# One of two low parts of the expert table's weights made by GpSimd, gathered rows' dot products with x in PSUM, and a ring of three PSUM banks in place of four

## The chip, the cores and the metric

One core of one Trainium2 chip runs the whole program in one launch. The metric is the device time of one execution in microseconds (us), the median over runs of the same kernel. TensorE (PE) does the matmuls, VectorE (DVE), ScalarE (ACT) and GpSimd (POOL) the elementwise work, SyncE (SP) issues most of the DMAs.

## The reference

Two transformer blocks follow each other over 512 tokens of width 1024, all in float32. The change lies in the second half of the first block, a layer of 16384 single-neuron experts (PEER):

```python
def chunk(xc):                                     # 128 tokens
    q = (xc @ wq).reshape(PEER_CHUNK, PEER_HEADS, 2, PEER_HALF)
    s = jnp.einsum('chpd,hpkd->chpk', q, subkeys)
    s1, i1 = lax.top_k(s[:, :, 0], PEER_TOPK)
    s2, i2 = lax.top_k(s[:, :, 1], PEER_TOPK)
    ...
    cs, ci = lax.top_k(cand, PEER_TOPK)
    eidx = jnp.take_along_axis(cidx, ci, axis=-1)  # 128 experts for a token
    g = jax.nn.softmax(cs, axis=-1)
    hid = jnp.einsum('cd,chkd->chk', xc, jnp.take(u_table, eidx, axis=0))
    a = jax.nn.gelu(hid, approximate=False) * g
    return jnp.einsum('chk,chkd->cd', a, jnp.take(v_table, eidx, axis=0))
```

Ahead of it stands attention (two kinds), behind it the second block: retention, a short convolution, gates and a feed-forward layer.

## The kernel before

**Units.** Every weight matrix is cut into 467 units of 128x1024 floats (`UNITS`). A unit is loaded by SP into one of six `raw` buffers, and float32 precision is made of two halves: ACT copies it to a rounded `wh` (`high`, L2370), and then the rest `wl = raw - wh` is taken (`low`, L1723 on DVE, L2753 on POOL). PE then runs three matmuls for each 128x128 tile: wh with the high part of the activations, wh with the low part, wl with the high part (`product`, L1266 to L1268). `wh` and `wl` have four buffers each, so the low part of unit u can be written once PE has finished unit u - 4. `low_on_pool` names the units whose low part POOL makes: 5 to 32 and 37 to 48. All others are DVE's.

**The order.** `timeline()` yields one long list of pieces, and every engine executes, in that order, those pieces for which it has a function. `Feed.next_unit` puts the high part of unit i + 3 and the low part of unit i + 2 ahead of the tiles of unit i. Work beside the matmuls is laid between them by costs (`Beside`, `side.start`, `yield 3.1`). No engine reorders anything: an instruction that waits holds up all behind it on its engine. A low part does not name who waits for it; PE waits for it before a unit's first tile.

**The first table's units**, 49 to 176 (`U_U` to `U_V`), are 128 units of the u table. The first 384 tokens (`ND`) go through the dense form: each unit gives 128 experts' hidden values for 384 tokens into a PSUM bank, and ACT applies the gelu out of that bank into `HID` (`hidden`, L2594), which SP stores. Banks 0 to 3 form a ring: unit number i (counted from 49) writes bank i % 4 and waits for the gelu of i - 4 (`u_bank`). In the same stretch these run beside the matmuls, mostly on DVE:

- the choice of experts for each of four groups of 128 tokens: `top`, `pair` (ten additions `CAN<-VAL`, then MAX8, FIND_INDEX8 and MATCH_REPLACE8), `gate` (softmax, with an exponential on ACT between two DVE steps), `chosen`, and `index` (the run of half-width operations on `D`, D1 in the code, 2048 down to 128 elements);
- the gate values spread over the dense form: `hot` (`OE`, a comparison) and `weigh` (`OM`) on DVE and ACT, `grid` on PE (L1611), a copy `GS` out of banks 6 and 7 on ACT. `OE` waits for the PE grid three before it;
- for the last 128 tokens, the sparse form: POOL gathers one row of the u table per token by an indirect DMA (`gather`, L2790, 116 of them, four buffers `GB`), and DVE takes the dot product of it with x (`dot`, L2031), where x lies in SBUF as `XT` (made by `rows`). `gather(n)` waits for `dot(n - 4)`.

POOL has nothing else to do there after its last `mod_part`. `gate_turn` transposes indices and gates into bank 4; banks 4 and 5 are otherwise idle after the last key product.

**The second table's units**, 177 to 304, accumulate into all eight banks; unit 177 takes the banks one after another (`v_bank`).

What touches what: the low parts are

```python
def low(i):                                       # on POOL; on DVE the same without s_low_p
    if low_on_pool(i):
        ...
        g.wait_ge(s_high, i + 1)
        wait_room(g, i)
```

Of the kernel before, what the change touches and what calls it, by code (L numbers as in the profile page):

```python
# [6 lines left out]
F32 = mybir.dt.float32  # L7
# [9 lines left out]
T = 512  # L17
# [34 lines left out]
def low_on_pool(i):  # L52
    return 5 <= i < U_WQ or U_WQ + 4 <= i < U_U

# [722 lines left out]
def build_program(nc, x, wts, ut, vt, skt, small, cst, dmat, augd, pos, adat, crow, un, out):  # L777
    ctx = ExitStack()
    with ctx:
# [32 lines left out]
        TB = [at(f"T{i}", 92 + 2 * i, [128, T], F32) for i in range(7)]  # L812
        P = [ctx.enter_context(nc.psum_tensor(f"P{i}", [128, T], F32)) for i in range(8)]
        G1, G2, GF, GM, GN, GE = (sm[:, 8 * i:8 * i + 8] for i in range(6))
# [444 lines left out]
        def _(e):  # L1259
# [54 lines left out]
            def u_bank(u):  # L1314
                i = u - U_U
                if i < 4:
                    p.wait_ge(s_qpl, 13 + i)
                else:
                    p.wait_ge(s_gelu, i - 3)
                return i % 4  # L1320

            def v_bank(d):
                if d < 4:
                    p.wait_ge(s_gelu, 125 + d)
                elif d == 4:
                    p.wait_ge(s_it, 3)
                    p.wait_ge(s_gtv, 3)
                elif d == 5:
                    p.wait_ge(s_keyc, 16)
                else:  # L1330
                    p.wait_ge(s_gs, 89 + d)
# [253 lines left out]
            def gate_turn(tb):  # L1585
                if tb == 0:
                    p.wait_ge(s_keyc, 16)
                else:
                    p.wait_ge(s_gtv, tb)
                    p.wait_ge(s_it, tb)  # L1590
                p.wait_ge(s_gate, tb + 1)
                for n, src in enumerate((IS[:, 0, :], IS[:, 1, :], GR[:, tb, :])):
                    t = e.transpose(P[4][:, n * 128:n * 128 + 128], src, ident[:, :])
                t.then_inc(s_gt, 1)
# [119 lines left out]
        def _(e):  # L1714
# [312 lines left out]
            def dot(n):  # L2027
                b = GB[n % 4]
                v.wait_ge(s_qpl, 18)
                v.wait_ge(d_row[n % 4], 16 * row_count(n))  # L2030
                e.tensor_tensor_reduce(out=b[:, :], in0=b[:, :], in1=XT[:, :], scale=1.0, scalar=0.0, op0=ALU.mult,  # L2031
                                       op1=ALU.add, accum_out=HS[:, n:n + 1]).then_inc(s_rows, 1)
# [333 lines left out]
        def _(e):  # L2366
# [220 lines left out]
            def hidden(i):  # L2587
# [311 lines left out]
```

## Time and profile before

| | |
|---|---|
| median of 3 runs | 2504.95 us (2503.87 to 2505.03) |
| profiled execution, span | 2502.2 us, 35461 instructions |
| PE busy | 2463.0 us (98%) |
| DVE busy | 1800.2 us (72%) |
| ACT busy | 1167.5 us (47%) |
| POOL busy | 541.9 us (22%) |
| chain that ended last | PE 92%, DVE 5%, ACT 1% |

The profile gives the profiled execution's span, from its first to its last instruction; its own time is not given apart, and the median of the runs stands 2.75 us above the span. How to read it: a busy PE is a matmul that is somewhere in the pipeline, so PE's rate is read from counts and from its waits, not from the share. The chain of waits follows back what the last instruction waited for. Units 49 to 176 run from 416 to 1003 us of the span, 4.16 us for a unit without a grid.

### The profile page before, as it was taken

How to read it: one execution, taken by the hardware profiler on the slowest of the kernel's cores; microseconds unless marked ns; L12 is line 12 of the kernel's file. 1: busy time of each engine (PE TensorE's matmuls, PEld its weight loads, DVE VectorE, ACT ScalarE, POOL GpSimd, SP SyncE). 2: the span in 40 equal slices, each digit the busy share in tenths (PEclk: the TensorE clock that was granted, in tenths of full speed). 3: DMA queues.
4: the chain of work that ended last, by engine and by line, in shares of the span. 5: the costliest groups of instructions: out<-in, count | busy, mean ns of one | idle time of the engine just before them, and what ended most of it. 6: DMA issues, size and time to landing. Idle time of an engine off the chain costs nothing.

```text
span 2502.2 us, 35461 instructions
## 1 busy us (share of the span) xinstructions
PE 2463.0 (98%) x13593; PEld 2236.5 (89%) x13593; DVE 1800.2 (72%) x3332; ACT 1167.5 (47%) x1970; POOL 541.9 (22%) x344
## 2 busy tenths in 40 slices
PE   8999999999999999999999999999999999999998
PEld 7788888999999999999999999788788888888887
DVE  7876678998998886799888987777786335533323
ACT  6555466467767786333333335444422223422222
POOL 3222165133222342365544400000000000000000
PEclk9999999999999999999999999999999999999999
DMA  4211345588888999999999972222374223233231
GB/s 169 69 61 43 118 144 173 188 313 317 323 297 296 343 395 336 390 389 390 390 393 391 389 272 75 84 97 84 131 266 163 96 91 108 76 101 101 97 98 42
DMA packets 191239, 519.15 MB, mean 207 GB/s; under 512 B 15896, under 2 KB 67096, under 8 KB 187872
## 3 DMA queue, kind: packets, MB, share of 16 engines
q1 hardware_dynamic: 154208, 382.66, 43.1%
q0 software_dynamic: 36864, 134.23, 14.5%
q8 instruction: 108, 1.77, 0.3%
q14 instruction: 59, 0.48, 0.1%
HBM read 464.34 MB, written 52.49 MB: 207 GB/s over the span
## 4 chain that ended last, share of the span: by engine, by line
PE 92%; DVE 5%; ACT 1%; issue 1%; DMA 0%; POOL 0%; DVEq 0%; SPq 0%; ACTq 0%
PE P L1266 28%; PE P L1268 28%; PE P L1267 28%; PE P L1611 2%; PE P L1273 1%; DVE wl L1723 1%; DVE D L1723 1%; ACT wh L2370 0%; PE P L1544 0%; PE P L1543 0%; PE P L1542 0%; PE P L1522 0%; PE P L1521 0%; PE P L1524 0%; PE P L1520 0%
## 5 line engine op out<-in xcount | busy, mean ns | idle before, releaser
L1266 PE MATMUL P<-XH,wh 128*128 128x512 f32 (+2 forms) x2272 | 847.2, 373 | 7.5 <-DVE wl L1723 5.3
L1268 PE MATMUL P<-XH,wl 128*128 128x512 f32 (+2 forms) x2272 | 824.8, 363 | 0.0
L1267 PE MATMUL P<-XL,wh 128*128 128x512 f32 (+2 forms) x2272 | 823.9, 363 | 0.0
L2370 ACT ACTIVATE wh<-raw 128x1024 fp32r<-128x1024 f32 x458 | 482.4, 1056 | 347.5 <-PE P L1268 339.9
L1723 DVE TENSOR_TENSOR wl<-raw,wh 128x1024 fp32r<-128x1024 f32 x418 | 507.6, 1222 | 74.1 <-ACT wh L2370 73.9
L1266 PEld LDWEIGHTS P<-XH,wh 128*128 128x128 f32 x2272 | 428.8, 189 | 53.3 <-DVE wl L1723 7.8
L1268 PEld LDWEIGHTS P<-XH,wl 128*128 128x128 f32 x2272 | 427.6, 188 | 47.5
L1267 PEld LDWEIGHTS P<-XL,wh 128*128 128x128 f32 x2272 | 428.7, 189 | 42.5 <-issue 1.9
L1266 PE MATMUL P<-AH,wh 128*128 128x384 f32 x1024 | 343.4, 335 | 1.7 <-DVE wl L1723 1.7
L1268 PE MATMUL P<-AH,wl 128*128 128x384 f32 x1024 | 342.6, 335 | 0.0
L1267 PE MATMUL P<-AL,wh 128*128 128x384 f32 x1024 | 342.6, 335 | 0.0
L2797 POOL DMA_INDIRECT GV<-vt,SI x128 | 212.3, 1659 | 196.8 <-DVE SUM L1726 173.5
L2790 POOL DMA_INDIRECT GB<-un,SI x116 | 160.0, 1379 | 380.9 <-DVE HS L2031 336.8
L1266 PEld LDWEIGHTS P<-AH,wh 128*128 128x128 f32 x1024 | 192.3, 188 | 2.6 <-DVE wl L1723 2.3
L1267 PEld LDWEIGHTS P<-AL,wh 128*128 128x128 f32 x1024 | 192.4, 188 | 0.0
L1268 PEld LDWEIGHTS P<-AH,wl 128*128 128x128 f32 x1024 | 192.3, 188 | 0.0
L1723 DVE TENSOR_TENSOR T<-P,T 128x512 f32<-128x512 f32 x47 | 32.5, 691 | 197.0 <-PE P L1268 191.8
L1726 DVE SCALAR_TENSOR_TENSOR SUM<-GV,HS,SUM 128x1024 f32<-128x1024 f32 x127 | 162.6, 1281 | 3.0
L2753 POOL TENSOR_TENSOR wl<-raw,wh 128x1024 fp32r<-128x1024 f32 x40 | 97.7, 2443 | 247.1 <-ACT wh L2370 245.2
L2031 DVE CUSTOM_DVE_ANT_0 GB<-GB,XT 128x1024 f32<-128x1024 f32 x116 | 140.6, 1217 | 3.1 <-DMA GB<-un,SI 2.9
L2573 ACT ACTIVATE OM<-OE,GTL 128x128 f16<-128x128 f16 x384 | 123.8, 432 | 0.5 <-DVE OE L1723 0.5
L2583 ACT ACTIVATE GS<-P 128x512 f32<-128x512 f32 x96 | 96.3, 1110 | 49.6 <-PE P L1611 49.2
(329 smaller groups left out, 3284.8 us busy)
## 6 DMA issues: line engine op xcount, KB each, us to landing
raw<-wts SPq DMA_DIRECT2D x211, 512.0 KB, 3.6
raw<-ut SPq DMA_DIRECT2D x128, 512.0 KB, 6.6
raw<-vt SPq DMA_DIRECT2D x128, 512.0 KB, 12.1
hdram<-HID SPq DMA_DIRECT2D x64, 384.0 KB, 4.7
gdram<-GS SPq DMA_DIRECT2D x24, 1024.0 KB, 6.4
GI<-gdram SPq DMA_DIRECT2D x16, 1536.0 KB, 16.5
HI<-hdram SPq DMA_DIRECT2D x32, 768.0 KB, 16.7
AWC<-adat SPq DMA_DIRECT2D x64, 256.0 KB, 5.0
```

The source lines that it names most:

```text
L1266: e.matmul(bank, wh[:, w], H, start=start, stop=False)
L1267: e.matmul(bank, wh[:, w], L, start=False, stop=False)
L1268: return e.matmul(bank, wl[:, w], H, start=False, stop=stop)
L1723: return e.tensor_tensor(dst, a, b, op)
L1726: return e.scalar_tensor_tensor(out=dst, in0=a, scalar=scalar, in1=b, op0=op0, op1=op1)
L2031: e.tensor_tensor_reduce(out=b[:, :], in0=b[:, :], in1=XT[:, :], scale=1.0, scalar=0.0, op0=ALU.mult, op1=ALU.add, accum_out=HS[:, n:n + 1 ...
L2370: return e.activation(dst, src, ACT.Copy)
L2573: t = e.activation(OM[n % 2][:, 1, r, :, o], OE[n % 3][:, 0, r, :, o], ACT.Copy, scale=GTL[n // 32 % 2][:, at_:at_ + 1])
L2583: e.activation(GS[g % 2][:, :, o:o + 4].rearrange("p i t -> p t i"), P[6 + n % 2][:, :].rearrange("p (t i) -> p t i", t=4), ACT.Copy, scal ...
L2753: e.tensor_tensor(WL[i % NW][:, :], RAW[i % NRAW][:, :], WH[i % NW][:, :].bitcast(F32), ALU.subtract).then_inc(s_low_p, 1)
L2790: e.indirect_dma_start(GB[n % 4][:, :], None, un, bass.IndirectOffsetOnAxis(ap=SI[:, n:n + 1], axis=0)).then_inc(d_row[n % 4], 16)
L2797: e.indirect_dma_start(GV[n % 6][:, :], None, table, bass.IndirectOffsetOnAxis(ap=SI[:, s:s + 1], axis=0)).then_inc(d_row[n % 6], 16)
```

## The change

Three things, which belong to each other:

1. `low_on_pool` also takes the units from `U_U + 6` = 55 up to `U_V - 7` = 170 that are odd: 55, 57, ..., 169, 58 of them. Their low parts go from DVE's list to POOL's, at the same place of the timeline.
2. The eight PSUM banks become one tensor `PS`, so that `XTP`, banks 4 and 5, can be read as one operand of 1024 columns. `rows` now also copies each half of `XT` there, and the 116 `dot`s of the first table read x from `XTP`. The 12 late dots still read `XT`.
3. The ring of the u units' results has banks 0 to 2, and `gate_turn` uses bank 3. At the second table's first unit the waits for banks 0 to 5 follow from that.

```diff
 def low_on_pool(i):
-    return 5 <= i < U_WQ or U_WQ + 4 <= i < U_U
+    return 5 <= i < U_WQ or U_WQ + 4 <= i < U_U \
+        or U_U + 6 <= i < U_V - 6 and i % 2 == 1
...
-        P = [ctx.enter_context(nc.psum_tensor(f"P{i}", [128, T], F32)) for i in range(8)]
+        PS = ctx.enter_context(nc.psum_tensor("PS", [128, 8 * T], F32))
+        P = [PS[:, T * i:T * i + T] for i in range(8)]
...
+        XTP = PS[:, 4 * T:6 * T]
...
             def u_bank(u):
                 i = u - U_U
-                if i < 4:
+                if i < 3:
                     p.wait_ge(s_qpl, 13 + i)
                 else:
-                    p.wait_ge(s_gelu, i - 3)
-                return i % 4
+                    p.wait_ge(s_gelu, i - 2)
+                return i % 3
 
             def v_bank(d):
-                if d < 4:
-                    p.wait_ge(s_gelu, 125 + d)
-                elif d == 4:
+                if d < 3:
+                    p.wait_ge(s_gelu, (127, 128, 126)[d])
+                elif d == 3:
                     p.wait_ge(s_it, 3)
                     p.wait_ge(s_gtv, 3)
-                elif d == 5:
-                    p.wait_ge(s_keyc, 16)
+                elif d < 6:
+                    p.wait_ge(s_rows, 1 + 128 - LATE)
...
                 tt(XT[:, w], P[7][:, :], XT[:, w], ALU.add).then_inc(s_qpl, 1)
+                v.wait_ge(s_qpl, 17 + half)
+                v.wait_ge(s_keyc, 16)
+                step(e.tensor_copy(XTP[:, w], XT[:, w]).then_inc(s_v, 1))
+                last["xtp"] = step.n
...
             def dot(n):
                 b = GB[n % 4]
-                v.wait_ge(s_qpl, 18)
+                v.wait_ge(s_v, last["xtp"])
                 v.wait_ge(d_row[n % 4], 16 * row_count(n))
-                e.tensor_tensor_reduce(out=b[:, :], in0=b[:, :], in1=XT[:, :], scale=1.0, scalar=0.0, op0=ALU.mult,
+                e.tensor_tensor_reduce(out=b[:, :], in0=b[:, :], in1=XTP, scale=1.0, scalar=0.0, op0=ALU.mult,
                                        op1=ALU.add, accum_out=HS[:, n:n + 1]).then_inc(s_rows, 1)
...
-                e.activation(HID[n % 2][:, i % 2, :], P[i % 4][:, 0:ND], ACT.Gelu).then_inc(s_gelu, 1)
+                e.activation(HID[n % 2][:, i % 2, :], P[i % 3][:, 0:ND], ACT.Gelu).then_inc(s_gelu, 1)
```

How the instructions stand on DVE around units 58 to 60, ahead of `sparse_index` (`SI`): `wl2` here is unit 58's low part, `wl3` unit 59's, `wl0` unit 60's. Before:

```order
L1723 TENSOR_TENSOR wl2_61<-raw4_53,wh2_57 128x1024
L1723 TENSOR_TENSOR D1_178<-ABH_183,IOP_185 128x2048
L1723 TENSOR_TENSOR D1_178<-D1_178,IF_176 128x2048
...
L1723 TENSOR_TENSOR IS_177<-D1_178 128x128
L1723 TENSOR_TENSOR wl3_62<-raw5_54,wh3_58 128x1024
L1723 TENSOR_TENSOR D1_178<-ABH_183,IOP_185 128x2048
...
L1723 TENSOR_TENSOR wl0_59<-raw0_49,wh0_55 128x1024
L1726 SCALAR_TENSOR_TENSOR CF_171<-IS_177 128x128
L2025 CAST SI_93<-CF_171 128x128
```

And with the change:

```order
L1726 TENSOR_TENSOR wl2_61<-raw4_53,wh2_57 128x1024
L1726 TENSOR_TENSOR D1_178<-ABH_183,IOP_185 128x2048
L1726 TENSOR_TENSOR D1_178<-D1_178,IF_176 128x2048
...
L1726 TENSOR_TENSOR IS_177<-D1_178 128x128
L1726 TENSOR_TENSOR D1_178<-ABH_183,IOP_185 128x2048
...
L1726 TENSOR_TENSOR wl0_59<-raw0_49,wh0_55 128x1024
L1729 SCALAR_TENSOR_TENSOR CF_171<-IS_177 128x128
L2032 CAST SI_93<-CF_171 128x128
```

The low part `wl3` between the two runs of `D1` is gone from DVE; all else keeps its place.

On POOL, from its last multiplication `AWB` of `mod_part`, seven low parts now stand ahead of the first gather, and from there on each pair of gathers or so has one between (before, the 116 gathers followed `AWB` directly):

```order
L2789 TENSOR_TENSOR AWB1_155<-AWB1_155,CBB_157 128x512
L2760 TENSOR_TENSOR wl3_62<-raw1_50,wh3_58 128x1024
L2760 TENSOR_TENSOR wl1_60<-raw3_52,wh1_56 128x1024
...
L2760 TENSOR_TENSOR wl3_62<-raw1_50,wh3_58 128x1024
L2797 DMA GB0_159<-un,SI_93 128x1024
L2797 DMA GB1_160<-un,SI_93 128x1024
L2797 DMA GB2_161<-un,SI_93 128x1024
L2797 DMA GB3_162<-un,SI_93 128x1024
L2760 TENSOR_TENSOR wl1_60<-raw3_52,wh1_56 128x1024
L2797 DMA GB0_159<-un,SI_93 128x1024
L2760 TENSOR_TENSOR wl3_62<-raw5_54,wh3_58 128x1024
```

A gather behind a low part starts after it, and a low part behind a gather waits for the dot that the gather waits for.

## Rows read from the trace of the kernel before

**Rows 1.** The page, busy time of each engine:
```profile
PE 2463.0 (98%) x13593; PEld 2236.5 (89%) x13593; DVE 1800.2 (72%) x3332; ACT 1167.5 (47%) x1970; POOL 541.9 (22%) x344
```
**Rows 2.** Busy time of each engine in four stretches; columns in the first line:
```profile
core 0: us, PE busy (x) PEld busy (x) DVE busy (x) ACT busy (x) POOL busy (x), PEclk, DMA share, GB/s
421.00:508.00 87.00, 84.08 (x484) 82.02 (x483) 82.16 (x273) 39.10 (x61) 9.04 (x7) 1.00 0.57 191
508.00:650.00 142.00, 142.00 (x954) 139.95 (x954) 131.24 (x305) 102.28 (x197) 47.62 (x32) 1.00 0.89 321
650.00:836.00 186.00, 186.00 (x1250) 183.30 (x1249) 167.61 (x411) 131.44 (x255) 43.61 (x33) 1.00 0.84 299
836.00:980.00 144.00, 144.00 (x1007) 141.29 (x1006) 124.49 (x198) 114.40 (x233) 60.98 (x45) 1.00 0.99 381
```
**Rows 3.** Waits in 421 to 1003 us; us in total, times, longest:
```profile
PEld P L1266 <- DVE wl L1723: 4.1, 5, 1.3
DVE OE L1723 <- PE P L1611: 30.8, 34, 2.1
DVE GB L2031 <- DMA GB<-un,SI: 2.9, 3, 1.9
```
**Rows 4.** Instruction groups by shape, 836 to 980 us; busy, mean ns, idle before, releaser:
```profile
L2031 DVE CUSTOM_DVE_ANT_0 GB<-GB,XT 128x1024 f32<-128x1024 f32 x48 | 58.1, 1220 | 3.1 <-DMA GB<-un,SI 2.9
L1723 DVE TENSOR_TENSOR wl<-raw,wh 128x1024 fp32r<-128x1024 f32 x31 | 37.8, 1221 | 0.8 <-ACT wh L2370 0.8
L1723 DVE TENSOR_TENSOR OE<-IOT,IT 128x1024 f16<-128x1024 f16 x34 | 23.4, 689 | 14.3 <-PE P L1611 14.2
L1723 DVE TENSOR_TENSOR OM<-OE,GTH 128x512 f16<-128x512 f16 x35 | 14.7, 419 | 0.0
```
**Rows 5.** The page, POOL's low parts:
```profile
L2753 POOL TENSOR_TENSOR wl<-raw,wh 128x1024 fp32r<-128x1024 f32 x40 | 97.7, 2443 | 247.1 <-ACT wh L2370 245.2
```
**Rows 6.** POOL and DVE in order of time, 278 to 291 us; start, duration:
```profile
280.95 2.63 POOL L2753 TENSOR_TENSOR wl<-raw,wh 128x1024 fp32r<-128x1024 f32 x1 [0.17 <-POOL wl L2753]
283.76 3.17 POOL L2753 TENSOR_TENSOR wl<-raw,wh 128x1024 fp32r<-128x1024 f32 x1 [0.17 <-ACT whr L2370]
287.10 3.18 POOL L2753 TENSOR_TENSOR wl<-raw,wh 128x1024 fp32r<-128x1024 f32 x1 [0.17 <-POOL wl L2753]
...
282.69 5.33 DVE L1723 TENSOR_TENSOR wlr<-raw,whr 128x1024 fp32r<-128x1024 f32 x2 [1.35 <-ACT whr L2370]
287.94 0.41 DVE L1723 TENSOR_TENSOR hT<-P,hT 128x256 f32<-128x256 f32 x1
288.27 2.55 DVE L1723 TENSOR_TENSOR T<-T,T 128x512 f32<-128x512 f32 x1
```
**Rows 7.** Instruction group by shape in 421 to 1003 us, the sum into `XT`:
```profile
L1723 DVE TENSOR_TENSOR XT<-P,XT 128x512 f32<-128x512 f32 x2 | 1.3, 672 | 0.0
```
**Rows 8.** POOL and DVE in order of time, 357 to 360 us:
```profile
357.60 2.40 POOL L2753 TENSOR_TENSOR wl<-raw,wh 128x1024 fp32r<-128x1024 f32 x1
...
358.80 0.29 DVE L1920 FIND_INDEX8 IDX<-VAL,S 128x8 uint32<-128x128 f32 x1
359.20 0.28 DVE L1922 MATCH_REPLACE8 S<-VAL,S 128x128 f32<-128x128 f32 x1
```
**Rows 9.** ACT in order of time, 437 to 492 us; start, duration:
```profile
449.00 1.06 ACT L2370 ACTIVATE wh<-raw 128x1024 fp32r<-128x1024 f32 x1
454.02 1.06 ACT L2370 ACTIVATE wh<-raw 128x1024 fp32r<-128x1024 f32 x1
462.34 1.05 ACT L2370 ACTIVATE wh<-raw 128x1024 fp32r<-128x1024 f32 x1
471.93 1.05 ACT L2370 ACTIVATE wh<-raw 128x1024 fp32r<-128x1024 f32 x1
484.18 1.06 ACT L2370 ACTIVATE wh<-raw 128x1024 fp32r<-128x1024 f32 x1
490.70 1.05 ACT L2370 ACTIVATE wh<-raw 128x1024 fp32r<-128x1024 f32 x1
```
**Rows 10.** DVE in order of time, 450 to 495 us:
```profile
452.90 1.23 DVE L1723 TENSOR_TENSOR D<-D,IF 128x2048 f16<-128x2048 f16 x1
454.16 1.48 DVE L1723 TENSOR_TENSOR D<-D 128x1024 f16<-128x1024 f16 x3
462.85 1.44 DVE L1723 TENSOR_TENSOR CAN<-VAL 128x128 f32<-128x128 f32 x10
473.13 0.23 DVE L1922 MATCH_REPLACE8 CAN<-CSV,CAN 128x80 f32<-128x80 f32 x1
485.69 1.22 DVE L1723 TENSOR_TENSOR D<-ABH,IOP 128x2048 f16<-128x2048 f16 x1
492.31 1.23 DVE L1723 TENSOR_TENSOR D<-D,IF 128x2048 f16<-128x2048 f16 x1
```
**Rows 11.** DMA issues in 836 to 980 us; KB, median us to landing:
```profile
GB<-un,SI POOLq DMA_INDIRECT x45, 9.0
```
**Rows 12.** ACT in order of time, around the gate's exponential and at the last unit:
```profile
436.99 0.49 ACT L2594 ACTIVATE HID<-P 128x384 f32<-128x384 f32 x1 [2.72 <-PE P L1268]
445.67 0.31 ACT L2557 ACTIVATE GR<-GR 128x128 f32<-128x128 f32 x1 [5.94 <-DVE GR L1723]
447.29 0.49 ACT L2594 ACTIVATE HID<-P 128x384 f32<-128x384 f32 x1
...
1002.83 0.47 ACT L2594 ACTIVATE HID<-P 128x384 f32<-128x384 f32 x1
```

More of the change, by code:

```diff
@@ L1586, in gate_turn @@
                 if tb == 0:
-                    p.wait_ge(s_keyc, 16)
+                    p.wait_ge(s_qpl, 16)
                 else:
@@ L1592, in gate_turn @@
                 for n, src in enumerate((IS[:, 0, :], IS[:, 1, :], GR[:, tb, :])):
-                    t = e.transpose(P[4][:, n * 128:n * 128 + 128], src, ident[:, :])
+                    t = e.transpose(P[3][:, n * 128:n * 128 + 128], src, ident[:, :])
                 t.then_inc(s_gt, 1)
@@ L2055, in gate_turn @@
                 q = slice(tb * 32, tb * 32 + 32)
-                src = P[4][:, 256:384].rearrange("p (n t) -> p n t", t=4)
+                src = P[3][:, 256:384].rearrange("p (n t) -> p n t", t=4)
                 rest = GTL[tb % 2][:, :].rearrange("p (n t) -> p n t", t=4)
@@ L2561, in gate_turn @@
                 copy(IT[:, 32 * tb:32 * tb + 32, :, :].rearrange("p n a t -> p a n t"),
-                     P[4][:, 0:256].rearrange("p (a n t) -> p a n t", a=2, t=4)).then_inc(s_it, 1)
+                     P[3][:, 0:256].rearrange("p (a n t) -> p a n t", a=2, t=4)).then_inc(s_it, 1)
             def weigh(n):
```

## The prediction

> **What bounds the kernel now.** I read the page first, then the busy times by stretch, the waits, and last the order in time on DVE, ACT and POOL. The page shows PE busy for 98% of the span [rows 1], so a gain can only come from a place where PE stands still. The stretches of the first table show where that is: in 508 to 980 us PE is busy without a gap, in 421 to 508 it lacks 2.9 us [rows 2], and the waits name the cause. The weight loads of a unit's first tile waited five times, 4.1 us in all, for a low part from DVE, and DVE is busy 82.2 of those 87 us [rows 2, 3]. The granted clock reads 1.00 in all four stretches, the upper of its two levels, 2.4 GHz [rows 2]. Two things are to be kept from this. First, 4.1 us (0.16% of the time) is all that a relief of DVE can give back. Second, around 455 to 500 us DVE sets PE's pace, so whatever makes DVE slower there is paid in full. A difference of 0.2%, 5.0 us, is about what a measurement of this kernel can tell from none.
>
> **The price of a low part on POOL.** DVE needs 1.22 us for one [rows 4], POOL 2.44 us [rows 5]. POOL's time costs nothing, since it has idle time; what costs is DVE's when both run. In 278 to 291 us they do. POOL made low parts back to back, and DVE's two `wlr`, the same shape as `wl`, took 5.33 us together, where 2.44 is their price alone; `T<-T,T` took 2.55 us. POOL's own took 2.63 to 3.18 us. But `hT<-P,hT`, one of whose inputs lies in PSUM, took 0.41 us in the middle of a POOL low part [rows 6]. So a DVE operation with two SBUF inputs that meets a POOL low part stands until that ends, and one with a PSUM input doesn't. A full meeting costs about 2.2 us: the two `wlr` lost 5.33 - 2.44 = 2.9 us, of which the first, begun at 282.69 while POOL's low part ended at 283.58, can have at most 0.9 and had about 0.7. The bounds are the `T<-T,T`'s 2.55 - 0.67 = 1.9 us (0.67 is the price of 512 columns, [rows 7]) and POOL's whole 2.44. I take 2.2. The search operations of the choice of experts are not held: FIND_INDEX8 and MATCH_REPLACE8 keep 0.28 to 0.29 us beside a POOL low part [rows 8]. The Trainium skill says the same in "SBUF — State Buffer", section "Who interferes with whom": an instruction of DVE with two SBUF inputs contends with a GpSimd instruction that reads SBUF, and the second to issue blocks fully. By that rule a moved low part saves 1.22 us and costs up to 2.44.
>
> **Part 1, seven low parts in 421 to 508 us.** Units 55 to 67 leave DVE: 7 x 1.22 = -8.5 us. POOL starts each when its `wh` is there, which is some 10 us before PE wants it, so PE will not wait for the odd units. Where they fall on DVE I read from ACT's rows [rows 9]: `wh` of unit 59 ends at 450.1, of 61 at 455.1, 63 at 463.4, 65 at 473.0, 67 at 485.2, 69 at 491.8 (the rows between belong to even units). At 450 and 455 DVE is in the run of `D`, at 463.4 in the ten `CAN<-VAL`, at 485 and 492 in `D` again, all with two SBUF inputs, and at 473 in MAX8 to MATCH_REPLACE8 [rows 10], which aren't held. So five full meetings, 5 x 2.2 = 11.0 us, one for nothing, and units 55 and 57, which fall into 430 to 441 us, mostly among MAX8 and the like, for which I choose 0.8 us together (0 to 4.4): +11.8.
>
> The two new copies of `XT` into PSUM stand in the same stretch. No row shows such a copy; nearest is the sum into `XT` with 0.67 us for the same 512 columns [rows 7], the lower end half of that (the half-width rate), the upper 0.9 with a wait for its own engine. I take 0.65 each: +1.3. Sum for DVE: -8.5 + 11.8 + 1.3 = +4.6 us, and since PE waits for DVE here, **+4.6 us**. The ends: if nothing but the fp32 operations meets POOL, 3.0 in place of 11.8, so -4.2, of which 4.1 are there to be had; with 2.44 for each meeting +6.
>
> **Part 2, 508 to 836 us.** Per two units DVE loses 1.22 us, and gains a meeting of 0 to 2.2; it has 29 us of idle time in 328 [rows 2], 31 us in the whole stretch by waiting for PE's grids [rows 3]. That is 0.8 us per pair, which with the 1.22 saved covers 2.0, nearly the dearest meeting. Cost **0**; if that cover is gone, the low parts of even units are late as in part 1.
>
> **Part 3, 836 to 980 us.** DVE is busy 124.5 of 144 us [rows 2]. 31 low parts [rows 4], 15 of which move: -18.3. A low part on POOL follows a gather, which starts at the end of a dot, so it meets what follows the dot: `OE` and `OM` (0.69 + 0.42) or the other low part, then a dot again, which is free. I take 1.7 for each, between 1.1 and 2.2: +25.5, which makes 131.7. Then the gathers: one behind a low part goes out up to 2.4 us later. They take 9.0 us to land [rows 11], and the dots have already waited 2.9 us for three of them [rows 3, 4], so there is hardly a lead left. With 1 us for each of 15, +15, DVE comes to 146.7 of 144. What overflows is late `OM` for PE's grids: **+3 us**, ends 0 and +7.
>
> **Part 4, the dots.** 116 of them read x from PSUM. `XT<-P,XT` takes 0.67 us per 512 columns, that is 1.34 for 1024 less one start, against 1.22 now [rows 4, 7]: I take 0, at most 0.1 each, on DVE alone. Without it each dot would meet POOL too. This part is the shelter, not a gain.
>
> **Part 5, the ring of three.** PE may run two units ahead of the gelu in place of three, 8.3 us in place of 12.5. The longest lag I can read: the gelu of unit 53 starts with PE's end at 437.0, unit 54 ends 4.16 us later at 441.1, and its gelu, behind the exponential that waits for DVE, ends at 447.8 [rows 12], 6.7 us after. It fits with 1.6 us to spare: 0. At the change of tables PE's second tile of unit 177 now waits for the gelu of unit 176, which ends 0.47 us after that unit [rows 12], three matmuls into unit 177: **+0.1 us**.
>
> **Sum**: 4.6 + 3 + 0.1 = +7.7 us. The profiled execution would go from 2502.2 to 2509.9, the median of the runs, which stands 2.75 above it, from 2504.95 to **2512.7 us**.
>
> **Rivals.**
> *A, half-width operations don't meet POOL.* No row shows an f16 operation beside a low part of POOL. If `D`, `OE` and `OM` don't hold what POOL needs, part 1 is -4.2, capped at -4.1, and part 3 ends well under 144 us: 2504.95 - 4.1 = 2501 us, not slower, and by this kernel's measure the same. For it speaks that `D` runs 2048 elements in 1.22 us [rows 10], twice the rate of fp32, so it is another mode; against it, that both of its inputs are in SBUF all the same, as those of the operations that were blocked. It decides from the point at which less than 1.2 us is lost per meeting. The Trainium skill's "Advanced Engine Details and Errata" lists this mode, 2x-1p, as one with a single read port; taken at its word, that is this rival. 0.22.
> *B, fewer meetings than I count.* When PE is held, `wh` moves too and the five meetings fall elsewhere; three in place of five is +0.2 in part 1, and without overflow in part 3 the time is 2504.95 + 0.2 to + 4.6, about 2507.5. 0.14.
> *C, the ring of three holds PE.* If DVE is 4.6 us late with the softmax sum and PE isn't yet, the 6.7 us become 11.3 against 8.3, +3 on top: 2515.7. It decides from 1.6 us of lag before unit 57. Against it: DVE is late by then only through the copies and unit 55. 0.05.
> *D, dots late for their rows throughout.* If POOL's queue, gather behind low part behind gather, sets the pace from 508 on, each pair of units lacks about 1 us: 40 us and more. 0.03.
> *E, faster by over 0.2%.* It needs over 5.0 us, and PE has 4.1 to give: 0.04, for what I can't see.
> The forecast keeps 0.52.
>
> **Range and chances.** It reaches down to rival A, 2501, and up to both upper ends together, 2504.95 + 6 + 7 + 0.1 = 2518. Slower by over 0.2% (above 2510.0): 0.52 + 0.05 + 0.03 = 0.60. Within: 0.22 + 0.14 = 0.36. Faster: 0.04.
>
> **What would show it.** In the profile after: POOL low parts of 2.4 us or more, 98 in all; `D` and `OE` on DVE with a mean well above 1.22 and 0.69 (were they unchanged, rival A holds); dots unchanged at 1.22 and never stretched; PE's waits for `wl` between 455 and 508 us about 8 to 9 us, all for even units; DVE's waits for `GB` rows up from 2.9 to 10 us or more, and PE waiting for `OM` after 836. I am wrong if the time is under 2510, above all if those waits of PE are gone.

## The result, and the profile after

| | before | changed |
|---|---|---|
| median of the runs | 2504.41 us (4 runs, 2502.93 to 2505.03) | 2514.8 us (4 runs, 2513.29 to 2515.82) |
| ratio, 95% interval | | 1.0041, 1.0028 to 1.0054 |
| span of the profiled execution | 2502.2 us | 2514.0 us |

The change costs 10.4 us, where I had forecast 7.7 (2512.7 us, range 2501 to 2518). The sign and the mechanism were right. Of the places that make the sum, one came near its size, one I had priced at nothing cost 6 us and one I had priced at 3 us cost nothing; the two errors partly cancel.

The page of the changed kernel, busy time of each engine and the group of GpSimd's low parts, against [rows 1, 5]:

```profile
PE 2466.4 (98%) x13593; PEld 2239.6 (89%) x13593; DVE 1825.0 (73%) x3276; ACT 1166.4 (46%) x1970; POOL 660.8 (26%) x402
...
L2760 POOL TENSOR_TENSOR wl<-raw,wh 128x1024 fp32r<-128x1024 f32 x98 | 244.1, 2491 | 345.5 <-ACT wh L2377 334.4
```

58 low parts have left DVE, 71 us of work at 1.22 us each, and yet DVE is busy for 24.8 us more. The busy times by stretch, changed kernel, against [rows 2], with the same columns:

```profile
421.00:508.00 87.00, 80.78 (x461) 79.67 (x460) 81.88 (x269) 38.75 (x60) 31.70 (x16) 0.98 0.49 171
508.00:650.00 142.00, 138.09 (x909) 135.74 (x908) 136.09 (x279) 96.81 (x186) 74.77 (x45) 0.99 0.87 306
650.00:836.00 186.00, 186.00 (x1250) 183.29 (x1249) 172.61 (x389) 131.00 (x254) 94.69 (x56) 1.00 0.85 303
836.00:980.00 144.00, 144.00 (x1008) 141.29 (x1007) 131.05 (x187) 113.15 (x229) 91.56 (x62) 1.00 0.98 379
```

PE lacks 6.2 us in the first stretch, where it lacked 2.9, and 3.9 us in the second, where it lacked nothing. From 650 on it has no gap at all. The waits of the changed kernel, 421 to 1012 us (us in total, times, longest), against [rows 3]:

```profile
PEld PS L1269 <- DVE wl L1726: 4.2, 2, 2.9
PE PS L1614 <- ACT GS L2590: 3.8, 2, 1.9
PE PS L1596 <- DVE IS L1726: 2.6, 1, 2.6
DVE OE L1726 <- PE PS L1614: 22.5, 16, 3.2
DVE GB L2038 <- DMA GB<-un,SI: 1.8, 2, 1.3
```

Where the time goes is plain when the end of every unit is laid beside the same unit's end in the kernel before. The changed kernel is 1.3 us behind before the change begins (at 52.8 us the granted clock stands at half for 3.4 us in the kernel before, and at 59.8 us for 6.8 us in this one; at 281.5 us it does so for 3.4 us in the kernel before alone); that is no part of its effect. Then:

| place | behind by | came from |
|---|---|---|
| unit 53 | 1.3 | earlier |
| the gate's first turn and unit 67 | 5.3 | +4.0, units 60 to 67 |
| unit 71 | 5.6 | +0.3, a grid whose weight load waited for `OM` |
| unit 83 | 7.7 | +2.1, one grid |
| unit 95 | 11.3 | +3.7, one grid |
| first tile of the second table | 11.3 | 0 in 650 to 1012 us |
| the end | 11.9 | +0.35 in unit 177, the rest in clock |

**What holds DVE.** DVE's groups in 421 to 1012 us, changed kernel (busy, mean ns, idle before):

```profile
L2038 DVE CUSTOM_DVE_ANT_0 GB<-GB,PS 128x1024 f32<-128x1024 f32 x116 | 139.5, 1209 | 1.8 <-DMA GB<-un,SI 1.8
L1726 DVE TENSOR_TENSOR OE<-IOT,IT 128x1024 f16<-128x1024 f16 x96 | 104.8, 1091 | 22.7 <-PE PS L1614 22.5
L1726 DVE TENSOR_TENSOR OM<-OE,GTH 128x512 f16<-128x512 f16 x96 | 77.3, 805 | 0.0
L1726 DVE TENSOR_TENSOR D<-ABH,IOP 128x2048 f16<-128x2048 f16 x8 | 11.9, 1493 | 0.1
```

`OE` took 689 ns and `OM` 419 before [rows 4]; now their means are 1091 and 805, over 96 of each, which is some 76 us of DVE's time. The dots, one of whose inputs is now in PSUM, took 1209 ns, 1220 before. GpSimd (POOL) and DVE in order of time, changed kernel, at six of the meetings:

```profile
451.34 2.72 POOL L2760 TENSOR_TENSOR wl<-raw,wh 128x1024 fp32r<-128x1024 f32 x1 [9.08 <-ACT wh L2377]
451.71 3.43 DVE L1726 TENSOR_TENSOR D<-ABH,IOP 128x2048 f16<-128x2048 f16 x1
...
464.59 1.22 DVE L1726 TENSOR_TENSOR wl<-raw,wh 128x1024 fp32r<-128x1024 f32 x1
464.82 3.21 POOL L2760 TENSOR_TENSOR wl<-raw,wh 128x1024 fp32r<-128x1024 f32 x1 [5.45 <-ACT wh L2377]
465.73 2.45 DVE L1729 SCALAR_TENSOR_TENSOR CF<-IS 128x128 f32<-128x128 f32 x1
465.86 0.60 PE L1269 MATMUL PS<-XH,wh 128*128 128x384 f32 x1 [2.60 <-DVE wl L1726]
...
565.81 3.13 DVE L1726 TENSOR_TENSOR OE<-IOT,IT 128x1024 f16<-128x1024 f16 x1
565.96 2.42 POOL L2760 TENSOR_TENSOR wl<-raw,wh 128x1024 fp32r<-128x1024 f32 x1
...
573.53 2.97 DVE L1726 TENSOR_TENSOR OM<-OE,GTH 128x512 f16<-128x512 f16 x1
573.84 2.36 POOL L2760 TENSOR_TENSOR wl<-raw,wh 128x1024 fp32r<-128x1024 f32 x1
574.07 0.64 PE L1614 MATMUL PS<-OE,OM 128*128 128x128 f16 x8
574.75 1.03 ACT L2590 ACTIVATE GS<-PS 128x512 f32<-128x512 f32 x1
576.60 0.62 PE L1614 MATMUL PS<-OE,OM 128*128 128x128 f16 x8 [1.89 <-ACT GS L2590]
...
629.53 2.96 DVE L1726 TENSOR_TENSOR OM<-OE,GTH 128x512 f16<-128x512 f16 x1
632.59 0.62 PE L1614 MATMUL PS<-OE,OM 128*128 128x128 f16 x8 [1.93 <-ACT GS L2590]
```

A held operation ends after GpSimd's low part by nearly its own duration: `D` by 1.08 us (1.22 alone), `OE` by 0.56 (0.69), `OM` by 0.30 (0.42). So it stands still until GpSimd is done and then runs at full speed. For `CF<-IS`, with 128 columns, that makes 2.45 us of 0.28: what is paid is what is left of GpSimd's duration, not a share of the operation's own.

It can also be the low part that stands. `wl` on DVE began at 464.59 and kept its 1.22 us; the low part that began at 464.82 took 3.21 us, against the 2.36 to 2.42 of those that met nothing of the kind. Which of two stands, the recorded starts alone don't tell. 14 of the held operations (12 `OM`, 2 `OE`) begin 0.14 to 0.32 us before the low part that holds them, as those at 565.81 and 573.53 do, while three other `OE` that begin 0.12 to 0.28 us ahead kept 0.69 us and the low part took 2.67 to 2.83. What decides is open.

The last rows also show how a wait's name can mislead. The profile names ACT's `GS` as what PE's second group of 8 grid matmuls waited for. But `GS` ended at 575.78, 0.82 us before they start. DVE's `OM` ended at 573.53 + 2.97 = 576.50, 0.10 us before. The grid waited for `OM`. At the other place it is the same: `OM` ends at 629.53 + 2.96 = 632.49, the grid goes on at 632.59. ACT makes a part of each `OM` too, but its parts had ended 4.9 and 3.9 us before these two grids go on.

**Why only two places of 96.** Each of the 96 groups of 8 grid matmuls needs one `OM` of DVE. I took the time from the end of each `OM` to the start of its group, its lead, and how much later than before the `OM` began in PE's own time (its start, less that of the kernel before, less what PE itself is behind). Then the lead left must be the lead before, less that delay, less what the `OM` itself was held:

| group (start, before) | lead before | began later by | `OM` held | left by this sum | lead after |
|---|---|---|---|---|---|
| 11 (568.9) | 4.46 | 3.9 | 2.55 | -2.0 | 0.10, PE's gap 2.11 |
| 21 (622.8) | 1.46 | 0.9 | 2.54 | -2.0 | 0.10, PE's gap 2.15 |
| 6 (546.7) | 8.42 | 2.1 | 2.60 | 3.7 | 3.69 |
| 26 (655.0) | 7.61 | 0.3 | 2.60 | 4.7 | 4.78 |
| 85 (941.0) | 3.93 | 3.4 | 0 | 0.5 | 0.51, the shortest in 836 to 980 us |

24 `OE` and 15 `OM` were held in all. A lead of 8 us swallows a delay and a held `OM` together. PE pays only where DVE was already late from meetings before (the `OE` at 565.81 is one) or the lead short, and the `OM` itself then met a low part. How close the others came is seen in the group at 514.5 us (start, before): its `OM` was held for 2.6 us too and ended 0.06 us before its grid, whose weight load waited 0.27 us for it: the +0.3 of unit 71.

**The clock.** The granted clock falls to half after two of PE's standstills, and not after two others. Windows of the changed kernel, each a standstill or what follows it:

```profile
462.90:465.90 3.00, 0.40 (x4) 0.08 (x2) 2.90 (x6) 1.43 (x2) 1.08 (x1) 1.00 0.00 0
466.00:469.40 3.40, 3.40 (x11) 3.40 (x12) 3.37 (x10) 0.00 (x0) 2.03 (x1) 0.50 0.70 229
574.50:579.90 5.40, 3.51 (x28) 3.37 (x26) 5.26 (x13) 3.33 (x7) 2.24 (x2) 1.00 0.99 326
630.40:632.60 2.20, 0.27 (x6) 0.12 (x4) 2.20 (x2) 1.03 (x1) 1.80 (x1) 1.00 0.99 376
633.20:636.60 3.40, 3.40 (x13) 3.40 (x12) 3.37 (x6) 3.35 (x7) 1.16 (x1) 0.51 0.41 117
498.80:504.00 5.20, 2.55 (x16) 2.24 (x15) 4.96 (x14) 1.13 (x2) 1.25 (x1) 1.00 0.98 370
```

3.4 us at the lower level, 1.2 GHz, are at most 1.7 us of lost work. That is the difference between the two grids: the gap was 2.11 us at unit 83 and 2.15 at unit 95, the loss 2.1 and 3.7. So of the 10.0 us that are lost between units 60 and 95, up to 3.4 may be clock. A fall isn't tied to a place either: in experiment 4 the clock fell after the grid of unit 83 (575.8 us, for 3.4 us) and not after that of unit 95.

### The profile page after: what moved, and what is told of

Its sections match the earlier page's. It is cut to its first block, busy times and chain, and to the rows that moved or that the text cites. A ratio compares the mean times of both kernels' runs of the same rounds, so it can differ in the third digit from the quotient of the medians.

```text
span 2514.0 us, 35464 instructions
## 1 busy us (share of the span) xinstructions
PE 2466.4 (98%) x13593; PEld 2239.6 (89%) x13593; DVE 1825.0 (73%) x3276; ACT 1166.4 (46%) x1970; POOL 660.8 (26%) x402
## 4 chain that ended last, share of the span: by engine, by line
PE 89%; DVE 7%; ACT 2%; DMA 1%; issue 1%; POOL 0%; DVEq 0%; SPq 0%; POOLq 0%; ACTq 0%
PE PS L1269 27%; PE PS L1271 27%; PE PS L1270 27%; PE PS L1614 2%; PE PS L1276 1%; DVE wl L1726 1%; DVE D L1726 1%; ACT wh L2377 1%; POOL wl L2760 0%; PE PS L1547 0%; PE PS L1546 0%; PE PS L1545 0%; PE PS L1525 0%; PE PS L1524 0%; DMA HI<-hdram 0%
## 5 line engine op out<-in xcount | busy, mean ns | idle before, releaser
L1269 PE MATMUL PS<-XH,wh 128*128 128x512 f32 (+2 forms) x2272 | 847.2, 373 | 8.5 <-DVE wl L1726 6.4
L1271 PE MATMUL PS<-XH,wl 128*128 128x512 f32 (+2 forms) x2272 | 824.8, 363 | 0.0
L1270 PE MATMUL PS<-XL,wh 128*128 128x512 f32 (+2 forms) x2272 | 824.1, 363 | 0.0
L1269 PEld LDWEIGHTS PS<-XH,wh 128*128 128x128 f32 x2272 | 429.6, 189 | 53.5 <-DVE wl L1726 7.9
L1271 PEld LDWEIGHTS PS<-XH,wl 128*128 128x128 f32 x2272 | 428.4, 189 | 47.8
L1270 PEld LDWEIGHTS PS<-XL,wh 128*128 128x128 f32 x2272 | 429.4, 189 | 42.6 <-issue 1.9
L1269 PE MATMUL PS<-AH,wh 128*128 128x384 f32 x1024 | 343.8, 336 | 1.8 <-DVE wl L1726 1.7
L1270 PE MATMUL PS<-AL,wh 128*128 128x384 f32 x1024 | 342.7, 335 | 0.0
L1271 PE MATMUL PS<-AH,wl 128*128 128x384 f32 x1024 | 342.7, 335 | 0.0
L2760 POOL TENSOR_TENSOR wl<-raw,wh 128x1024 fp32r<-128x1024 f32 x98 | 244.1, 2491 | 345.5 <-ACT wh L2377 334.4
L1270 PEld LDWEIGHTS PS<-AL,wh 128*128 128x128 f32 x1024 | 192.8, 188 | 0.0
L2038 DVE CUSTOM_DVE_ANT_0 GB<-GB,PS 128x1024 f32<-128x1024 f32 x116 | 139.5, 1209 | 1.8 <-DMA GB<-un,SI 1.8
L1726 DVE TENSOR_TENSOR OE<-IOT,IT 128x1024 f16<-128x1024 f16 x96 | 104.8, 1091 | 22.7 <-PE PS L1614 22.5
```

The costliest lines, as they stand in the source:

```text
L1269: e.matmul(bank, wh[:, w], H, start=start, stop=False)
L1270: e.matmul(bank, wh[:, w], L, start=False, stop=False)
L1271: return e.matmul(bank, wl[:, w], H, start=False, stop=stop)
L1726: return e.tensor_tensor(dst, a, b, op)
L2038: e.tensor_tensor_reduce(out=b[:, :], in0=b[:, :], in1=XTP, scale=1.0, scalar=0.0, op0=ALU.mult, op1=ALU.add, accum_out=HS[:, n:n + 1]).th ...
L2760: e.tensor_tensor(WL[i % NW][:, :], RAW[i % NRAW][:, :], WH[i % NW][:, :].bitcast(F32), ALU.subtract).then_inc(s_low_p, 1)
```

## The experiments

Two theories stand against each other. **L**: a low part on GpSimd holds the two-operand DVE operation that it meets; the loss hangs on where it falls, and x in PSUM shelters the dots. **S**, with **P** and **G** as its kin: every low part costs its share, or another part of the change does. Each kernel was timed beside the kernel before on the same chip (its medians: 2504.61 us for experiments 1 to 4, 2503.90 for 5 and 7 to 9, 2503.73 for 6 and 10). Each edit is to `low_on_pool` alone, in the changed kernel, where it ends as below, or (experiments 2 and 9) in the kernel before:

```
    return 5 <= i < U_WQ or U_WQ + 4 <= i < U_U \
        or U_U + 6 <= i < U_V - 6 and i % 2 == 1
```

The order of all of DVE's other work is the same in the changed kernel and in every run that is an edit of it (2916 instructions without the low parts); only low parts come or go. What moves with an edit is time, so that a meeting that one edit removes can still come back somewhere else. U_U is 49.

**1. Without the low parts.** The last line goes; x in PSUM and the ring of three stay.

```
-        or U_U + 6 <= i < U_V - 6 and i % 2 == 1
```

> The change without its first part: POOL makes no low part of the first table, but the dots read x from PSUM, the two copies into PSUM stand there and the ring has three banks. Theory L (DVE operations with two SBUF inputs stand still while POOL makes a low part, and that makes PE wait): 2504.4 + 0.5 us, 0 to +1.5, D, OE and OM back at 1.22, 0.69 and 0.42 us. Rival R (the ring of three and the copies are what costs): +6 to +10 us, and PE's waits for ACT's GS stay.

Measured: 2505.47 us, ratio 1.0003 (0.9994 to 1.0012). `OE` 688 ns, `OM` 418, dots 1212. The low parts are the loss, within the interval; parts 4 and 5 of the prediction, the dots and the ring, cost nothing that these medians can tell, as forecast. The trace does show something small: this kernel falls back by 0.7 us in units 59 and 60, ahead of the gate's turn, and by 0.8 in unit 177, where the ring of three waits for the last gelus.

**2. The low parts without x in PSUM.** The kernel before, with the line added.

```
+        or U_U + 6 <= i < U_V - 6 and i % 2 == 1
```

> The first part of the change alone, on the kernel before: 58 odd low parts on POOL, the dots read x from SBUF, the ring has four banks. Theory L: the dots now meet POOL's low parts too, their mean goes from 1.21 to 1.6 us or more (many over 3 us), and the time is above that of the change, 2520 to 2560 us. Rival P (PSUM for the dots does nothing): dots at 1.22 us, 2514 us or, without the ring of three, less.

Measured: 2524.3 us, ratio 1.0078 (1.0063 to 1.0093): twice the loss of the whole change. DVE's dots, by the instruction groups of 421 to 1012 us:

```profile
L2032 DVE CUSTOM_DVE_ANT_0 GB<-GB,XT 128x1024 f32<-128x1024 f32 x116 | 172.2, 1490 | 7.7 <-DMA GB<-un,SI 7.7
```

PE's waits of the same kernel in the same stretch:

```profile
PE P L1612 <- issue: 7.6, 7, 3.5
...
PE P L1612 <- ACT GS L2584: 3.0, 2, 1.9
```

With both inputs in SBUF the dots lose 32.7 us (1490 against 1209 ns, 116 times), and PE's grids stand for 10.6 us in place of 3.8. So part 4 is the shelter that the prediction called it, worth some 9.3 us once the low parts are there (+19.7 against +10.4), though I had expected the dots to be held harder, to a mean of 1.6 us or more.

**3. Only the first seven, units 55 to 67.**

```
-        or U_U + 6 <= i < U_V - 6 and i % 2 == 1
+        or U_U + 6 <= i < U_U + 20 and i % 2 == 1
```

> The change with only units 55 to 67 on POOL, seven low parts. Theory L: the part of the loss that the trace after shows up to unit 70 and nothing behind: +4 us (+2 to +6), waits of PE for DVE's wl and IS in 455 to 510 us, no wait of PE for GS. Rival R: as in the change, +8 to +10.

Measured: 2506.2 us, ratio 1.0007 (0.9998 to 1.0016); no wait of the grids. Less than half of the +4 expected, and under its range of +2 to +6. In the trace this kernel is 0.3 us ahead at unit 53 and 1.7 behind from the gate's turn on, 2.0 us lost. Up to 1.7 of that is clock: PE stands 2.6 us before unit 60, as in the changed kernel, and the granted clock is at half for 3.4 us after it.

**4. Only from unit 69 on.**

```
-        or U_U + 6 <= i < U_V - 6 and i % 2 == 1
+        or U_U + 20 <= i < U_V - 6 and i % 2 == 1
```

> The change with only units 69 to 169 on POOL, 51 low parts. Theory L: PE's waits up to unit 68 as in the kernel before (about 4 us, already in its time), and the two waits within grids, which in the trace after came with units 83 and 95 and cost 2.1 + 3.7 us with the clock's fall: +5.5 us (+2 to +8). The sum of this run's loss and of the one with the first seven low parts is that of the whole change if the parts don't depend on each other. Rival R: as in the change, +8 to +10.

Measured: 2513.24 us, ratio 1.0040 (1.0026 to 1.0053), +8.6 against the +5.5 expected, over its range of +2 to +8. What 3 fell short by is here: the low part of unit 69 met `D<-D,IF` (3.30 us at 493.56), and the wait of PE's weight load before unit 67 grew from 0.60 us to 2.69. So the stretch to the gate's turn is not the first seven units' alone. The two sets together, 1.6 + 8.6 = 10.2, make the 10.4 of the whole.

**5. Four of the 58 go back to DVE.** Units 83, 85, 95 and 97, whose low parts ran beside the held `OE` and `OM` of the two late grids.

```
-        or U_U + 6 <= i < U_V - 6 and i % 2 == 1
+        or U_U + 6 <= i < U_V - 6 and i % 2 == 1 and i - U_U not in (34, 36, 46, 48)
```

> The changed kernel with 54 of its 58 new low parts still on GpSimd; those of units 83, 85, 95 and 97 go back to VectorE. In the trace of the changed kernel these four run at 565.96, 573.84, 620.82 and 629.83 us, and beside each an OE or OM operation of VectorE takes 2.75 to 3.13 us; TensorE then waits 3.8 us in two places for the GS that follows. Theory L (what the change costs behind unit 69 is these places alone: a low part on GpSimd holds an f16 operation of VectorE with two operands in SBUF, ScalarE's GS comes late, and TensorE's grid matmuls wait, each time with a half-clock window or not): some 6 of the 10.3 us come back, 2508.5 us, and no wait of TensorE for GS between 560 and 640 us. Theory S (spread: every meeting costs a little and the whole 58 add up): 4 of 58 are worth 0.7 us, 2514 us. If other low parts then meet OE or OM in the same places, the waits for GS move and the time stays over 2512.

Measured: 2509.39 us, ratio 1.0021 (1.0012 to 1.0030): about half of the loss is gone with 4 of 58 low parts. Busy times of this kernel in 508 to 650 us (columns as in [rows 2]):

```profile
508.00:650.00 142.00, 141.87 (x942) 139.66 (x941) 138.96 (x289) 99.00 (x189) 69.24 (x43) 1.00 0.89 317
```

Its PE waits in 421 to 1012 us:

```profile
PE PS L1269 <- DVE wl L1726: 3.6, 2, 2.6
PE PS L1596 <- DVE IS L1726: 2.6, 1, 2.6
PE PS L1269 <- ACT HID L2601: 0.3, 1, 0.3
```

No grid matmul of PE waits any more, though 20 `OE` and 16 `OM` are still held, some 70 us of DVE's time.

**6. Eight go back.** Units 59, 63, 67 and 69 too, which met `D<-ABH,IOP`, `CF<-IS`, `D<-D,IF` and `D<-D`.

```
-        or U_U + 6 <= i < U_V - 6 and i % 2 == 1
+        or U_U + 6 <= i < U_V - 6 and i % 2 == 1 \
+        and i - U_U not in (10, 14, 18, 20, 34, 36, 46, 48)
```

> The changed kernel with 50 of its 58 new low parts on GpSimd; beside units 83, 85, 95 and 97 (whose return gave 2509.4 us, 5.4 of the 10.4) units 59, 63, 67 and 69 go back to VectorE too. In the trace of the changed kernel these run at 451.34, 464.82, 488.53 and 497.49 us, and beside them D<-ABH,IOP took 3.43 us, CF<-IS 2.45, D<-D,IF 3.30 and D<-D 3.53 us; TensorE then waited for wl at 462.9 and for IS at 498.8. Theory L (the loss hangs on where a low part falls, not on how many there are): nearly all of the rest goes, 2504.5 to 2506.5 us. Theory S (every meeting costs its share): 50/58 of the 10.4 us would stay, 2513. If four more low parts of VectorE (1.22 us each) delay the index operations by themselves, 2507 to 2508, with TensorE's waits for wl at 460 to 495 us longer than the 4.1 us of before.

Measured: 2505.25 us, ratio 1.0004 (0.9995 to 1.0013). Groups of DVE, 421 to 1012 us:

```profile
L1727 DVE TENSOR_TENSOR OE<-IOT,IT 128x1024 f16<-128x1024 f16 x96 | 97.0, 1010 | 19.2 <-PE PS L1615 19.0
L1727 DVE TENSOR_TENSOR OM<-OE,GTH 128x512 f16<-128x512 f16 x96 | 79.3, 826 | 0.0
```

Its PE waits in the same stretch:

```profile
PE PS L1270 <- DVE wl L1727: 2.6, 3, 1.5
PE PS L1597 <- DVE IS L1727: 0.4, 1, 0.4
PE PS L1615 <- DVE OM L1727: 0.4, 1, 0.4
PE PS L1270 <- ACT HID L2602: 0.3, 1, 0.3
```

This is what settles it. 50 of the 58 low parts are still on GpSimd, `OE` and `OM` still lose some 70 us, and the time is that of the kernel before. Theory S would have 2513. The eight low parts carry the loss of the change, within what the interval can tell. (In the trace 0.5 us are lost from unit 53 to the second table and 0.6 in unit 177; one `OM`, for the grid at 515.24, was late by 0.4.)

**7. Only from unit 99 on.**

```
-        or U_U + 6 <= i < U_V - 6 and i % 2 == 1
+        or U_U + 50 <= i < U_V - 6 and i % 2 == 1
```

> The changed kernel with low parts on GpSimd only from unit 99 to 169 (36 of the 58). My prediction priced the stretch behind unit 108 at +3 us, the trace of the change showed no loss behind unit 95. Theory L: TensorE has no wait left there that the low parts could lengthen, since its wait for GS arises only where a grid pair follows closely on the OE and OM that it needs; 2504.5 to 2505.5 us, ratio 1.000. Theory S (every meeting costs): 36/58 of 10.3 is +6.4 us, 2511. The step of my prediction by itself: 2507.6.

Measured: 2506.94 us, ratio 1.0008 (0.9999 to 1.0017), 36 low parts moved. In its trace the second table starts 0.9 us later than in the kernel before; most of the rest of the profiled span's 2.7 us comes behind that, in the granted clock (at half for 3.4 us at 1523.3, which the kernel before has not; experiment 1, without any of these low parts, has it too). Not quite the 2504.5 to 2505.5 expected, far from S's 2511, and the median can't tell it from my prediction's step (2507.6); the trace can: PE is busy for 144.88 of the 145 us from 845 to 990.

**8. All 116.** Every unit from 55 to 170.

```
-        or U_U + 6 <= i < U_V - 6 and i % 2 == 1
+        or U_U + 6 <= i < U_V - 6
```

> The changed kernel with the low parts of all units 55 to 170 on GpSimd (116 in place of 58), VectorE makes none there. Theory L: 116 low parts of about 2.5 us and 128 gathers of 1.2 us take GpSimd 440 us of 590, and twice as many meetings hold OE, OM and the index operations; the waits of TensorE for GS and IS come more often: +15 to +40 us against before, 2520 to 2545. Theory R (VectorE's relief counts: 116 x 1.22 = 141 us off VectorE against 58 x 1.22 in the change): back to 2505 to 2510 us.

Measured: 2538.43 us, ratio 1.0134 (1.0119 to 1.0150), three times the loss for twice the low parts. DVE's `OE` among the groups of 421 to 1012 us:

```profile
L1726 DVE TENSOR_TENSOR OE<-IOT,IT 128x1024 f16<-128x1024 f16 x96 | 152.9, 1592 | 24.4 <-PE PS L1614 20.7 <-issue 3.6
```

Its PE waits there:

```profile
PE PS L1596 <- DVE IS L1726: 11.1, 3, 9.4
PE PS L1614 <- issue: 7.7, 9, 2.5
PE PS L1269 <- ACT HID L2601: 7.3, 1, 7.3
PE PS L1614 <- ACT GS L2590: 4.9, 3, 1.9
```

And one meeting, POOL and DVE in order of time:

```profile
472.16 2.39 POOL L2760 TENSOR_TENSOR wl<-raw,wh 128x1024 fp32r<-128x1024 f32 x1 [1.25 <-ACT wh L2377]
472.21 2.43 DVE L2032 CAST SI<-CF 128x128 uint32<-128x128 f32 x1
```

DVE makes no low part here at all, and the kernel is the slowest of all: relief of DVE is no argument once what relieves it also holds it. The wait of 7.3 us for `HID` is rival C in the flesh: the second exponential of the gate starts at 488.1 us (480.8 before) because DVE is late with its sum, the gelu stands behind it on ACT, and PE has three banks and not four. In the change itself that wait never came.

**9. Four units that should meet nothing.** The kernel before, with low parts of units 56, 57, 64 and 65 on GpSimd: their `wh` is ready while DVE is in MAX8 and FIND_INDEX8.

```
-    return 5 <= i < U_WQ or U_WQ + 4 <= i < U_U
+    return 5 <= i < U_WQ or U_WQ + 4 <= i < U_U \
+        or i in (U_U + 7, U_U + 8, U_U + 15, U_U + 16)
```

> The kernel before with the low parts of only units 56, 57, 64 and 65 made on GpSimd. In its trace the weights of these four are ready when VectorE is in its runs of MAX8 and FIND_INDEX8, so a low part of GpSimd there should meet none of the two-operand operations that it holds, and TensorE's waits for these units' low parts (part of 4.1 us in 5 waits between 421 and 1012 us) should go. Theory L: 2501 to 2503.5 us, ratio 0.9985 to 0.9995. Theory G (VectorE pays for any low part of GpSimd, wherever it falls): 2504.5 or above.

Measured: 2500.86 us, ratio 0.9989 (0.9980 to 0.9998), the fastest of all. Busy times of its first stretch (columns as in [rows 2]):

```profile
421.00:508.00 87.00, 86.08 (x502) 85.33 (x501) 81.98 (x279) 41.30 (x66) 19.89 (x12) 1.00 0.60 206
```

Its PE waits in 421 to 1012 us:

```profile
PE P L1267 <- DVE wl L1724: 0.9, 1, 0.9
PEld P L1267 <- DVE wl L1724: 1.2, 1, 1.2
```

PE's weight loads wait 1.2 us for `wl` in place of 4.1 [rows 3], and the gate's turn comes 3.8 us earlier, of which 0.6 were there at unit 53, ahead of the edit. The other 3.2 are what was had of the 4.1 us that the prediction named as all there was to be had; the median gives 3.0. It is a gain of 0.1%, below the 0.2% that I called measurable for one pair of medians; with 11 runs against 27 the interval just leaves out 1. Two of the four did meet something: one low part (467.07) stood behind DVE's `wl` and took 3.36 us, which PE did not wait for, and one (471.23) held a `wl` of DVE to 2.25 us.

**10. The same four, with x in PSUM and the ring of three.**

```
-        or U_U + 6 <= i < U_V - 6 and i % 2 == 1
+        or i in (U_U + 7, U_U + 8, U_U + 15, U_U + 16)
```

> The changed kernel (x in PSUM for the dots, three banks) with the low parts of units 56, 57, 64 and 65 alone on GpSimd, in place of its 58. With the kernel before these four gave 2500.9 us, ratio 0.9989, and the change without its low parts was 1.0003. Theory L: x in PSUM and the ring of three stay neutral where TensorE has no slack either, 2501 to 2502.5 us, V0 no more than 1 us behind that of the four units alone. If the ring of three or the copy of x into PSUM costs once TensorE's other waits are gone (TensorE of the four units alone was busy for 86.1 of the 87 us from 421 to 508), 2503 us or more, with a wait of TensorE for ACT HID or DVE IS in that stretch.

Measured: 2503.12 us, ratio 0.9996 (0.9987 to 1.0005). The second table starts 1.4 us later than with the four units alone, where I had expected 1 at most, and PE waits 2.0 us for `wl` and 0.3 for `HID`. The median lies just over the 2503 at which my second expectation began, but the wait that it named, for `HID` or `IS` in 421 to 508 us, isn't there; the interval overlaps that of experiment 9. Of the 2.1 us that the trace lies behind experiment 9's after unit 177, 1.2 come by the gate's turn. The ring of three has no wait there, and the two copies of x into PSUM take 0.695 us each, 1.4 together, on DVE where DVE sets the pace; that they are the 1.2 us is likely and not shown. The rest comes at the change of tables: from the end of unit 176 to the end of unit 177 each of the nine kernels with three banks loses 0.3 to 0.9 us, and the two others with four banks (experiments 2 and 9) lose nothing.

## Why the prediction was right, and where it was wrong

| step | predicted | measured |
|---|---|---|
| price of a full meeting | 2.2 us (1.9 to 2.44) | 2.1 to 2.2 in part 1, up to 2.6 behind it |
| part 1, 421 to 508 us | +4.6 | +4.0, of it up to 1.7 clock |
| part 2, 508 to 836 us | 0 | +6.0 |
| part 3, 836 to 980 us | +3 | 0 |
| part 4, dots in PSUM | 0 | 0 (experiment 1) |
| part 5, ring of three | +0.1 | +0.35 (0.3 to 0.9 in other kernels) |
| sum | +7.7 | +10.4 in the medians |

**The price of a meeting** held. `D<-ABH,IOP` went from 1.22 to 3.43 us, `D<-D,IF` from 1.22 to 3.30, `CF<-IS` from 0.28 to 2.45. An `OM` paid up to 2.6 us (0.42 to 3.01), over my upper bound, because it begins some 0.3 us before the low part and is held all the same. Rival A, that f16 operations don't take part, was plainly wrong: `OE`, `OM` and `D` are all f16. The Trainium skill's "Advanced Engine Details and Errata", by whose entry for that mode rival A stood, lists that mode with one read port; if that were to mean that the shared port stays free, these rows contradict it. What the Trainium skill's "SBUF — State Buffer", section "Who interferes with whom", says of two SBUF inputs is borne out by all of them, and by the dots from PSUM, which kept 1209 ns. What it says of order, that whoever issues first keeps the ports and the other blocks fully, these traces bear out only in part: one of the two does stand fully, but by the recorded starts it was 14 times the one that began first.

**Part 1** came out in its meetings, and in its size partly by luck. Five full meetings were forecast, for units 59, 61, 63, 67 and 69, none for 65, and little for 55 and 57. The trace has the five: +2.2 at 451.71, +2.1 at 457.16 (a `D<-D`), +2.2 at 465.73, +2.1 at 489.14 and +2.1 at 497.85; at 477.57 and 439.86 the low part ran beside MAX8 and FIND_INDEX8, which kept 0.24 us; and a `wl` at 433.68 lost 0.3. Only the signature was off: I expected PE's waits for `wl` at 8 to 9 us. They stayed at 4.2, since PE was held there by the index `IS` as well, 2.6 us, and lost up to 1.7 us more to the clock, which my sum didn't have. The sum has a slip, too: it takes seven low parts off DVE, but the fifth meeting is that of unit 69, an eighth one. With its 1.22 us saved as well the sum is +3.4; for the first seven alone, with four meetings, it is +2.4, and experiment 3 has +1.6 in the median and 2.0 in the trace, up to 1.7 of it clock.

**Part 2 is the step that failed.** I set DVE's mean idle time per pair of units, 0.8 us, against the mean cost of a meeting and found them even. PE doesn't wait for a mean. It waits for one `OM`, and what protects it is that `OM`'s own lead, between 0.4 and 12 us. Where 3.4 and 6.4 us of delay fell on leads of 1.46 and 4.46 us, PE stood; everywhere else the lost time of DVE cost nothing, but for the 0.3 us of unit 71. Experiments 5 and 6 show it: take these places and the four of part 1 away, and some 70 us of held operations are free.

**Part 3** counted the gathers wrong. DVE's busy time in 836 to 980 us came to 131.05 us, 131.7 forecast. But the 15 us for rows that land late didn't come: DVE's wait for `GB` fell from 2.9 to 1.8 us. A DVE that is held takes the dot later too, and by then the row is there; that fits, and no run tests it. Without them DVE had room, and the shortest lead there was 0.51 us. That is not much: the 0 of this part is by luck of placing as much as by margin, and experiment 8 overran it: there PE is busy for 138.64 of the 145 us from 845 to 990. So did experiment 2, where the dots are held too: PE is busy for 140.21 of the 144 us from 836 to 980.

**The size.** 2512.7 against 2514.8 is closer than the working deserves, and that is luck: +3 too much in one part, 6 too little in another, and a part 1 whose 4.0 us are up to 1.7 clock.

## What to carry to other kernels

Moving work to GpSimd does not cost its duration there but the meetings it makes: a VectorE operation with two SBUF inputs that it meets stands until it ends, however small, unless it is the GpSimd operation that stands. So ask not how many low parts move but which operation each will meet and what lead that operation's reader has; choose the few places beside work that isn't held (MAX8, FIND_INDEX8, an operand in PSUM). And do not set a mean of idle time against a mean cost: list the leads of the results that the bounding engine waits for, one by one, and look at the shortest.

## What the runs showed of the hardware that I had not expected

- A held operation pays GpSimd's whole remaining time even when it is tiny: a 128-column operation went from 0.28 to 2.45 us, and in experiment 8 a cast with a single input, both sides in SBUF, took 2.43 us beside a low part, where it takes 0.23 alone. One of the two copies of x into PSUM ran beside a low part in the change (433.07) and kept 0.69 us.
- After PE stood still for 2.9 us (462.9) and for 2.15 us (630.4) its granted clock was at 0.50 and 0.51 for 3.4 us; after 3.0 us at 498.8 and 2.1 at 574.5 it stayed at 1.00. What decides between them these runs don't show.
- GpSimd's low part is little slowed on the whole: its mean was 2491 ns over 98 in the change and 2443 over 40 before. Single ones take up to 3.42 us (at 750.73); there, as at 464.82 (3.21), a `wl` of DVE that had just begun kept its 1.22 us and the low part stood.
